# v token-major: activations as stationary operand, 256 weight columns moving, and a reordered opening

## The reference

```python
h = rms_norm(x, norm_w) * (1 + scale) + shift
proj = h @ w_in                       # xbc 2048, z_m, dt 32, u, v, z_g, gl_m, gl_g: 1024 each
xbc = silu(dwconv5(xbc_raw))          # then dt = softplus(...), a chunked scan per direction
v = layer_norm(gelu(v_raw), ln_w, ln_b)
s = einsum('gts,bnsgc->bntgc', w_sp, vg) + b_sp   # mixes the 128 tokens of a chunk, per group of 128 channels
y_g = gelu(u_raw) * s * silu(z_g)
x = x + gate * ((sig(gl_m) * (y_m @ w_out_m) + sig(gl_g) * (y_g @ w_out_g)) @ w_out)
```

## Time and profile before

| | us |
|---|---|
| median of 3 runs | 1466.22 (1465.71 to 1467.43) |
| the profiled execution | 1466.37 |
| its span, first to last instruction | 1464.4 |
| TensorE busy with products | 1444.1 (99%) |
| GpSimd, VectorE, ScalarE busy | 1025.2, 991.8, 485.4 |
| mean granted TensorE clock | 0.995 of full |

### The profile page before, as it was taken

One profiled execution on the slowest core, in us unless ns is written; L12 is line 12 of the kernel. 1 busy time (PEld: TensorE's weight loads), 2 busy tenths in 40 slices (PEclk: granted clock), 3 DMA queues, 4 the chain that ended last, 5 costly groups with the idle time before them and its releaser, 6 DMA issues.

```text
span 1464.4 us, 26742 instructions
## 1 busy us (share of the span) xinstructions
PE 1444.1 (99%) x10003; PEld 1397.8 (95%) x10003; DVE 991.8 (68%) x1451; ACT 485.4 (33%) x1115; POOL 1025.2 (70%) x1437
## 2 busy tenths in 40 slices
PE   7999999999999999999999999999999999999996
PEld 5899999899999999999999999989999999999996
DVE  5666566674777778888868765667567885867234
ACT  4431233312766423101244423341256661320111
POOL 2688765596655489898868876648765556979762
PEclk9999999999999999999999999999999999999998
DMA  9122434123566465444332233321347664453222
GB/s 360 48 77 73 128 87 139 51 73 101 163 182 188 122 267 189 145 157 144 115 132 73 75 110 109 125 76 58 101 116 198 165 175 183 158 187 116 73 74 85
DMA packets 108940, 190.29 MB, mean 130 GB/s; under 512 B 10656, under 2 KB 72224, under 8 KB 107424
## 3 DMA queue, kind: packets, MB, share of 16 engines
q1 hardware_dynamic: 38400, 139.65, 28.5%
q10 hardware_dynamic: 70432, 49.11, 11.5%
HBM read 170.58 MB, written 18.15 MB: 129 GB/s over the span
## 4 chain that ended last, share of the span: by engine, by line
PE 97%; DMA 1%; SPq 1%; DVE 1%; POOL 0%; issue 0%; ACT 0%; DVEq 0%; POOLq 0%
PE acc L514 84%; PE X L747 2%; PE X L714 2%; PE X L739 2%; PE X L778 1%; PE X L674 1%; DMA w_st<-in_wts 1%; PE X L758 1%; PE acc L524 1%; SPq L395 1%; PE acc L633 0%; PE X L563 0%; DVE xr L1818 0%; PE X L721 0%; PE X L696 0%; PE X L766 0%
## 5 line engine op out<-in xcount | busy, mean ns | idle before, releaser
L459 POOL CAST w_hi<-w_st 128x256 fp32r<-128x256 f32 x712 | 408.4, 588 | 414.9 <-PE acc L514 193.3
L464 POOL TENSOR_TENSOR w_lo<-w_st,w_hi 128x256 fp32r<-128x256 f32 x712 | 655.9, 931 | 0.0
L514 PE MATMUL acc<-h_hi,w_hi 128*128 128x320 f32 x2000 | 466.7, 315 | 1.8 <-ACT h_hi L945 1.8
L514 PE MATMUL acc<-h_lo,w_hi 128*128 128x320 f32 x2000 | 456.0, 309 | 0.4 <-DVE h_lo L1374 0.4
L514 PE MATMUL acc<-h_hi,w_lo 128*128 128x320 f32 x2000 | 455.6, 309 | 0.0
L514 PEld LDWEIGHTS acc<-h_hi,w_hi 128*128 128x128 f32 x2000 | 330.8, 188 | 12.6 <-issue 8.5
L514 PEld LDWEIGHTS acc<-h_lo,w_hi 128*128 128x128 f32 x2000 | 334.1, 188 | 1.1 <-DVE h_lo L1374 0.9
L514 PEld LDWEIGHTS acc<-h_hi,w_lo 128*128 128x128 f32 x2000 | 334.4, 188 | 0.0
L1517 DVE SCALAR_TENSOR_TENSOR cv<-raw,convw_sb,cv 128x642 f32<-128x642 f32 x128 | 135.7, 1060 | 4.5
L1302 DVE SCALAR_TENSOR_TENSOR ada_acc<-ada_st,sc,ada_acc 128x512 f32<-128x512 f32 x112 | 103.4, 962 | 1.8
L1515 DVE TENSOR_SCALAR cv<-raw,convw_sb 128x642 f32<-128x642 f32 x32 | 27.6, 863 | 72.4 <-ACT raw L1104 72.2
(11 more groups left out here) (248 smaller groups left out, 2086.9 us busy)
## 6 DMA issues: line engine op xcount, KB each, us to landing
w_st<-in_wts SPq DMA_DIRECT2D x178, 512.0 KB, 3.6
cum_bc<-cum_dram ACTq DMA_DIRECT2D x80, 256.0 KB, 4.8
ada_st<-in_wada SPq DMA_DIRECT2D x33, 512.0 KB, 4.2
ex_bc<-ex_dram ACTq DMA_DIRECT2D x64, 128.0 KB, 3.4
ada_pre<-in_wada SPq DMA_DIRECT2D x15, 512.0 KB, 13.3
mga_dram<-c_buf SPq DMA_DIRECT2D x16, 320.0 KB, 4.7
xf<-xf_dram SPq DMA_DIRECT2D x4, 1280.0 KB, 7.1
mga<-mga_dram SPq DMA_DIRECT2D x2, 2560.0 KB, 9.4
```

The source lines that it names most:

```text
L459: nc.gpsimd.tensor_copy(w_hi[:, slot, cols], w_st[:, slot, cols]).then_inc(s_pool, 1)
L464: nc.gpsimd.tensor_tensor(w_lo[:, slot, cols], w_st[:, slot, cols], f(w_hi[:, slot, cols]), ALU.subtract).then_inc(w_split, 1)
L514: last = mm(a[:, hf, 0:n1], w[:, s, cols], x[:, k, hf * HALF:hf * HALF + n1], start=(k == 0 and n == 0), stop=(k == KC - 1 and n == 2))
```

## The change

v is made token-major at once. For a pair of v tiles (p = 4 and 5, 10 and 11, 16 and 17, 23 and 24) the stationary operand is a 128-token chunk of h, the moving one 128 columns of each of the two weight tiles; the first tile of the pair holds k = 0..3 of both, the second k = 4..7. Four chunks stand in the two banks of one accumulator, the fifth in the upper half of X[1] or X[3]. Two GELUs write `v_tok` after the pair. Accumulators are counted by `acc_no`, which counts a pair once. In layer 1 the raw tiles are dt and three conv tiles (`NRAW = 3`). The x transposes stand at other places. In the opening, job 0's and job 1's products are cut in halves with the statistics between, and GpSimd makes the dt tile's two parts itself.

```diff
-V_AT = (2, 5, 8, 11, 14, 17, 20, 24)
+V_AT = (4, 5, 10, 11, 16, 17, 23, 24)
-RAWT, NRAW = 4, 2
+RAWT, NRAW = 4, 3
+def acc_no(t):
+    L, p = divmod(t, N_TILES)
+    return L * (N_TILES - len(V_AT) // 2) + p - sum(q <= p for q in V_AT[1::2])
-X_AT = [(p + 2, 8 if p + 1 in V_AT else 5) for p in CONV_AT[8:]]
-VT_AT = [(p + 1, 6 if p < RAWT else 3) for p in V_AT]
+X_AT = [(p + 2, 8) for p in CONV_AT[8:13]] + [(25, 3), (25, 5), (25, 8)]
+V_BANK = (1, 1, 3, 1)
     def acc_of(t):
-        return acc[t % 2]
+        return acc[acc_no(t) % 2]
...
+            if p in V_AT:
+                n, half = KC * P // 2, V_AT.index(p) % 2
+                dst = dst.rearrange("p (t n) -> p t n", t=2)
+                src = wts[at - half:at - half + 2, :, n * half:n * (half + 1)].rearrange("t p n -> p t n")
...
+        split(1, 16, None)
+        dt_st, dt_hl = (w[:, 1, :].rearrange("p (k n) -> p k n", n=P) for w in (w_st, w_hi))
+        nc.gpsimd.tensor_copy(dt_hl[:, :, 0:32], dt_st[:, :, 0:32]).then_inc(s_pool, WQ)
+        pool.wait_ge(s_pool, base + 2 * WQ)
+        nc.gpsimd.tensor_tensor(dt_hl[:, :, 32:64], dt_st[:, :, 0:32], f(dt_hl[:, :, 0:32]), ALU.subtract)\
+            .then_inc(w_split, WQ)
...
+        def v_tile(t, half, ready=None, hooks=()):
+            j = V_AT.index(t % N_TILES) // 2
+            if half == 0:
+                acc_ready(t)
+                if j > 0:
+                    pe.wait_ge(v_made, KC // 2 * (t // N_TILES) + j)
+                elif ready is not None:
+                    pe.wait_ge(hpre_ready, 8 * (ready[2] + 1))
+            a, s = acc_of(t), t % 2
+            for i in range(KC // 2):
+                k = KC // 2 * half + i
+                if i % 2 == 0:
+                    pe.wait_ge(w_split, WQ * t + 3 + i // 2)
+                if ready is not None:
+                    for r in ready[0:2]:
+                        pe.wait_ge(r, 8 * ready[2] + k + 1)
+                for c in range(NCH):
+                    out = X[V_BANK[j]][:, 2 * P:4 * P] if c == NCH - 1 else \
+                        a[:, c // 2, 2 * P * (c % 2):2 * P * (c % 2 + 1)]
+                    for n, (w, x) in enumerate(((w_hi, h_hi), (w_lo, h_hi), (w_hi, h_lo))):
+                        last = mm(out.rearrange("p (t n) -> p t n", t=2), x[:, k, P * c:P * (c + 1)],
+                                  w[:, s, :].rearrange("p (t k n) -> p k t n", t=2, n=P)[:, i, :, :],
+                                  start=(k == 0 and n == 0 and c % 2 == 0),
+                                  stop=(k == KC - 1 and n == 2 and (c % 2 == 1 or c == NCH - 1)))
...
         def opening(hi, lo):
-            pe.wait_ge(dtw_ready, 1)
+            pe.wait_ge(w_split, 2 * WQ)
             for k in range(KC // 2):
                 dt_chunk(1, k, hi, lo)
-                if k == 1:
-                    first_mm(3)
-            first_tp(3)
+                if k < 2:
+                    (first_mm, first_tp)[k](3)
...
+                if a == 1:
+                    pe.wait_ge(v_made, KC // 2 * L + V_BANK.index(3) + 1)
...
-        keep_pace(12)
-        first_mm(0)
+        keep_pace(17)
+        first_mm(0, range(DTG))
         stat_mm(0)
+        first_mm(0, range(DTG, KC))
+        keep_pace(2)
+        stat_bc(0)
+        first_mm(1, range(DTG))
         first_tp(0)
-        stat_bc(0)
-        first_mm(1)
-        keep_pace(3)
+        keep_pace(2)
+        first_mm(1, range(DTG, KC))
+        keep_pace(2)
         first_tp(1)
...
+                if X_AT[j][0] > V_AT[-1]:
+                    pe.wait_ge(v_made, KC // 2 * (L + 1))
...
-        row_copy(0)
         root(0)
+        row_copy(0)
...
                 if p in V_AT:
-                    j = V_AT.index(p)
-                    if j == 0:
-                        act.wait_ge(tmT_ready, L + 1)
-                    elif j > 1:
-                        act.wait_ge(tp_ready, 16 * L + tp_no("v", j - 2))
-                    if L > 0 and p < RAWT:
-                        evacuated(act, t)
-                        for v, cols in ((0, slice(0, CTX)), (1, slice(CTX, TOK))):
-                            last = A(c_buf[j][:, cols], c_buf[3 - p % 2][:, cols], ACT.Gelu_apprx_tanh,
-                                     bias=bsh[:, p, v:v + 1])
-                        last.then_inc(vraw_ready, 1)
-                    else:
-                        free(t, A(halves(c_buf[j % 2]), acc_of(t)[:, :, 0:HALF], ACT.Gelu_apprx_tanh))
-                    if L > 0 and j == 1:
-                        conv_tanh(1)
-                        dt_log()
-                    if j > 0:
-                        conv_tanh(CONV_AT.index(p - 1))
+                    j, half = divmod(V_AT.index(p), 2)
+                    if L > 0 and p == RAWT:
+                        conv_tanh(NRAW - 1)
+                    if half == 1:
+                        g = slice(2 * j, 2 * j + 2)
+                        free(t, A(v_tok[:, g, 0:NCH - 1, :].rearrange("p g c n -> p c g n"),
+                                  acc_of(t)[:, :, :].rearrange("p b (c g n) -> p (b c) g n", c=2, n=P),
+                                  ACT.Gelu_apprx_tanh))
+                        A(v_tok[:, g, NCH - 1, :], X[V_BANK[j]][:, 2 * P:4 * P].rearrange("p (g n) -> p g n", n=P),
+                          ACT.Gelu_apprx_tanh).then_inc(v_made, 1)
                     copies(p + 1)
                     continue
                 i = CONV_AT.index(p)
                 if L > 0 and i < NRAW:
-                    if i == 1:
-                        raw_conv(1, p)
-                        conv_tanh(0)
-                        dt_exp()
+                    if i > 0:
+                        raw_conv(i, p)
+                        conv_tanh(i - 1)
+                        (dt_exp, dt_log)[i - 1]()
                         copies(p + 1)
...
-                for a in {10: (0, 1), 11: (2,), 12: (3,), 13: (4, 5), 14: (6,), 15: (7, 8)}.get(i, ()):
+                for a in {10: (0, 1), 11: (2,), 12: (3,), 13: (4,), 14: (5, 6), 15: (7, 8)}.get(i, ()):
                     a_unit(a)
```

More of the change, by code:

```diff
@@ L88 @@
 STANDS = sorted([(at, "a", n) for n, at in enumerate(A_AT)] + [(at, "x", n) for n, at in enumerate(X_AT)]
-                + [(at, "v", n) for n, at in enumerate(VT_AT)] + [(PBB_AT, "pbb", 0)]
+                + [(PBB_AT, "pbb", 0)]
                 + [(at, "sp", n) for n, at in enumerate(SP_AT)] + [(at, "b", n) for n, at in enumerate(B_AT)])
-TPS = [(what, n) for at, what, n in STANDS if what in ("x", "v")]
 def stands(p):
     return [(at[1], what, n) for at, what, n in STANDS if at[0] == p]
-def tp_no(what, n):
-    return TPS.index((what, n)) + 1
 JOBS_FIRST = [(0, q, h) for h in (0, 1) for q in (1, 0)]
@@ L467, in _ @@
         base = own.n
[L468 to L474, removed]
+        split(0, 16, None)
+        split_hi(0, 0)
+        for q in range(WQ):
+            if q + 1 < WQ:
+                split_hi(0, q + 1)
+            split_lo(0, q, base + q + 1)
+        split(1, 16, None)
[4 more added lines that the diff above has]
+            .then_inc(w_split, WQ)
         with pool.Fori(1, DEPTH * N_TILES // 2) as i:
@@ L487, in _, with acc_ready @@
         mm = nc.tensor.matmul
+        def acc_ready(t):
+            pe.wait_ge(acc_free[acc_no(t) % 2], acc_no(t) // 2)
+        def v_tile(t, half, ready=None, hooks=()):
[22 more added lines that the diff above has]
+                                  stop=(k == KC - 1 and n == 2 and (c % 2 == 1 or c == NCH - 1)))
+                    if i == KC // 2 - 1 and c == NCH - 1:
+                        last.then_inc(tile_done, 1)
+                    for at, hook in hooks:
+                        if (at == 2 * i + 1 and c == 2) or (at == 2 * i + 2 and c == NCH - 1):
+                            hook()
         def tile(t, hi, lo, ready=None, hooks=(), more=0):
             if t >= 2:
-                pe.wait_ge(acc_free[t % 2], t // 2)
+                acc_ready(t)
             for k in range(KC):
@@ L579, in first_mm @@
                 pe.wait_ge(row_out, 3)
-            for k in range(KC):
+            for k in ks:
                 j = k % DTG
-                if n == 0 and k == DTG:
-                    keep_pace(2)
                 if j == 0:
@@ L587, in first_mm @@
                           start=(k < DTG), stop=(k >= DTG))
-            last.then_inc(row_mm, 1)
+            if k == KC - 1:
+                last.then_inc(row_mm, 1)
         def first_tp(n):
@@ L830, in _ @@
                     dt_tile(T0 + p, *rows, more=more)
-                else:
-                    tile(T0 + p, *rows, ready=(hhi_ready, h_ready, L) if L > 0 and p == RAWT else None,
-                         hooks=hooks, more=more)
+                elif p in V_AT:
+                    v_tile(T0 + p, V_AT.index(p) % 2, hooks=hooks,
+                           ready=(hhi_ready, h_ready, L) if L > 0 and p < RAWT + 2 else None)
+                else:
+                    tile(T0 + p, *rows, hooks=hooks, more=more)
                 if p == (3, 7)[L]:
@@ L933, in _ @@
```

(5 more changed lines are left out.)

54 lines of the change are left out of this document (23 added, 31 removed).

## The result

The changed kernel takes **1472.02 us** (median of 7 runs, 1471.20 to 1472.70), the kernel before in the same session 1466.27 (7 runs, 1465.59 to 1467.43). The ratio is 1.0037 with an interval of 1.0025 to 1.0049: slower by 5.75 us. I had said 1464.5, with a range of 1456 to 1469. The profiled execution took 1472.30 with a span of 1470.2, against a span of 1464.4 before, so 5.8 us are to be found in the trace.

The account below looks back on a forecast made before the run. TensorE's products, filling 99% of the span, were taken to bound the kernel. The terms -8.8 + 0.5 - 3.7 + 7.2 + 1.6 + 1.4 = -1.8 us, from 1466.3, gave 1464.5 us, range 1456 to 1469.

Parts of the forecast that it names:

- step 2: v products: a pair's 120 products of 256 columns at 117.9 ns take 14.15 us, +0.5 us for eight pairs.
- step 4: Layer 1, tile 7: TensorE waits for the accumulator that the pair's GELU frees, behind tanh(2) and a table load, +7.2 us.
- step 5: End of each layer's convolutions: tile 25 waits 0.65 us for bt, x groups just fit; +1.4 us in two layers.
- 1 transposes of v: Both layers: sixteen groups of v transposes at 0.55 us leave TensorE's path, -8.8 us.
- 3 opening: Opening: dt tile ready sooner and last modulation job earlier, so tile 0's second half starts sooner, -3.7 us.
- 4 clock behind it: Layer 1, after the stop at tile 7: TensorE's clock is low for a while, +1.6 us, bounds 0 and 2.
- v tiles wanting three quarters: v tiles need three of four split weight quarters at their start; GpSimd at 5.8 us a tile keeps up, 0 us.
- What costs nothing: Split quarters for v tiles, weights in 2 KB pieces, extra raw tile on ACT, bigger LayerNorm delay: no added time.
- B: Rival: no wait in layer 1, as the GELU gets through in time or tile 7's accumulator is another; 1455.7 us, chance 0.18.
- C: Rival: v products with two runs of columns take more than 117.9 ns; at 128 ns, 1474.2 us; chance 0.10.
- D: Rival: the opening isn't shortened, because the jobs' weights come when they come; 1468.2 us, chance 0.10.

Follow-up runs that it names:

- e4: The kernel before with only the changed kernel's opening put in, v keeping its transposes: 1463.07 us, ratio 0.9979.
- e1: The changed kernel with tanh(2) behind the GELU of layer 1's first v pair on ACT instead of ahead of it: 1461.4 us, ratio 0.9969.
- e5: The changed kernel with 66 added float32 products of 256 columns between tiles 6 and 7 of layer 1: 1489.87 us, ratio 1.0158.
- e8: The changed kernel with 18 added float32 products of 256 columns between tiles 6 and 7 of layer 1: 1469.64 us, ratio 1.0027.
- e2: The changed kernel with x group 5's transposes and copy at the end of tile 22 instead of in tile 25: 1468.5 us, ratio 1.0015.
- e7: The changed kernel with the moves of e1 and e2, and unit 6 behind the last convolution on DVE: 1457.22 us, ratio 0.9939.
- e3: The changed kernel with v products reading 256 consecutive columns instead of two runs of 128, v's values wrong: 1471.75 us, ratio 1.0040.
- e12: The changed kernel with six more GpSimd subtractions from the moment the last tile begins: 1471.27 us in a single run.

## Why the prediction was wrong

The mechanisms were there, nearly all of them. Four sizes were wrong, all to the same side: 2.0 us in step 2, 2.1 in step 4 (of them 1.28 for a table load priced at nothing, and 1.3 in the clock, less 0.5 elsewhere), 2.6 in step 5 and 0.6 counted at nothing, 7.3 of the 7.5 us by which 1464.5 missed.

| step of the prediction | said | measured | shown by |
|---|---|---|---|
| 1 transposes of v | -8.8 | -8.8 | trace |
| 2 products of v | +0.5 | +2.5 | trace: 8 x (14.39 - 14.08) |
| 3 opening | -3.7 | -3.8 | trace, e4 |
| 4 stop in layer 1 | +7.2 | +8.0 | e1 |
| 4 clock behind it | +1.6 | +2.9 | e1, e5, e8 |
| 5 end of convolutions | +1.4 | +4.0 | e2, e7 |
| v tiles wanting three quarters | 0 | +0.6 | trace |
| sum | -1.8 | +5.4 | span: +5.8 |

**1** held. **3** held in size (-3.76 for -3.7), and the half clock went too. The two limits of the second half came within 0.1 us of each other, and the one that ended last was the job's result (37.74) and not h_pre (37.64), which the prediction had named. The first half gave nothing: h_hi(0) starts at 25.05 instead of 25.09, where 24.2 was hoped for.

**2** failed by its size. "I take 117.9, the row with the same width and loads" took a row from another stage, the last tile, and the bound of 128 was kept for the two runs of columns, which e3 showed to cost nothing. Every v product of every form took 120.0 ns. The row of the convolution stage itself would have given that: 146.6 ns for 320 columns, less 64 columns at 2.4 GHz (26.7), is 119.9. What separates the two places isn't settled: columns, order, roles, order and roles together, GpSimd and the transfers have each been ruled out.

**4** is where the list was right and one entry was missing. The taps ended 25.13 us after the pair's start (I had 25.17). But ACT needed 4.49 us from there to the release of TensorE, and I had 3.2. I had counted one table load. The load for tanh(2) stood 8 us ahead of its tanh in the kernel before (792.50, then 800.46), and I took it for hidden again. In the changed kernel the load came behind the wait, at 795.67: 1.28 us on the path. ACT's program has one more wait there, for tile 4, between dt_log and tanh(2); whether that is what moved the load, no run shows. The other side, TensorE's want of tile 7, was 0.4 later than worked out, partly by step 2. 25.13 + 4.49 - 21.59 = 8.03. Of the Trainium skill (ScalarE: Activation LUTs, What ACT_TABLE_LOAD costs) the drain of some 1.38 us behind each load is again not seen: 797.72 + 1.28 = 799.00, and the GELU starts at 799.01. By the page the two loads would have cost 2.8 us more than they did.

The clock term took its size from stretches of 3.2 us in the opening and a cost of 1.6. Here it stayed at half for some 6 us of tile 7, and +1.6 became +2.9 (2.7 of it the clock's own, by e8), outside the bound of 2.

**5** failed at "I count that as just enough". Group 5's transposes, ACT's copy, the store and DVE's write form a chain through one of two xo buffers, with a DMA store in it that took 4.51 us. From 227.19 the store alone used up nearly all of the 5 us that I had between the first group and the third. It cost 3.5 us in two layers by e2's medians, 3.1 by its traces. The bt wait, sized at 0.65 a layer, cost less: burst 6 was 0.4 late, and e7 puts it at 0.5 in layer 0. Both together are 4.2 us by the medians of e1 and e7; the +4.0 of the table is 3.5 and 0.5. A step that fits "just enough" deserved the length of its longest part, and the store's was to be had from the trace.

**What costs nothing** was nearly right. I took GpSimd's mean of 5.8 us a tile. In the convolutions of layer 0 its tiles take from 4.2 to 8.0 us; two in a row, from 93.95 and 101.33, take 7.4 and 8.0, longer than TensorE's 7.04, so it falls behind there, and tile 10 paid some 0.6 us. The mean over the kernel hid the stage.

**Rivals.** B (no wait in layer 1) did not hold. e1 makes its case, and came to 1461.4 instead of 1455.7, since the other sizes were off there too. C is ruled out as a mechanism (two runs), and D by the opening. None of them was the case that came: the forecast's own terms, all but the opening and the transposes above what was taken, and two above their bounds (the clock, 2.9 against 2, and the second wait, 4.0 against 3). I had spread them to 1468, as if they would err to both sides. They didn't: each price had been taken from another stage (the last tile, the opening, the mean over the kernel) or, for the store, from none.

## What to carry to other kernels

When a buffer is released by a later step than before, write out everything that stands ahead of the new releaser on its engine, each table load included, and put the release first: here two lines moved gave back 10.6 us. A stop of TensorE can cost more than its length; this one of 8.0 us cost 10.9. Where a chain goes through a small ring of buffers with a store in it, take the store's full time from issue to landing, and move its first user as early as its data allow; and read the pace of a helper engine in the stage concerned, not over the whole kernel.

## What the hardware showed that I had not expected

- A float32r product of 256 columns had 120.0 ns from start to start in all of the convolution phase, whatever its form and with the other engines at work or not, and 117.9 in the last tile, with GpSimd at work beside it (2.83 us for 24 products in e12) or not (2.82).
- After 8.0 us without a product the granted clock was 0.50 from 800 to 806 us, and 18 products of float32 data in the gap (7.8 us) kept it at 1.00. The Trainium skill (TensorE: Matmul & The Clock Gate, Part 1: The HAM clock gate) names 1.2 GHz and 2.4 GHz as the two states of the gate. The levels seen, 0.50 and 1.00 of full, agree.
- A product with float32 data on 256 columns took two passes of 0.216 us, 0.43 together, 3.6 times that of a float32r product of the same width (0.12).
- A table load stood 8 us ahead of its activation in one kernel (792.50, tanh at 800.46) and behind the wait, on the path (795.67, tanh at 796.96), in the other, though both switch from Ln to tanh.
